# The last turn of an expert loop written out behind the loop, and a new order for the end of the kernel

## What is computed

```
for e in range(N_EXPERTS):                       # 32
    gate, up = jnp.split(z @ w_gate_up[e], 2, axis=-1)
    y = y + combine[..., e:e + 1] * ((jax.nn.silu(gate) * up) @ w_down[e])
...
return rms_norm(x + y, final_norm_g)
```

## Time and profile before

| | us |
|---|---|
| median of three runs (all: 896.52, 898.11, 900.98) | 898.11 |
| the profiled execution, its own time | 898.83 |
| the span of its trace, first to last instruction | 897.0 |
| first step of the loop begins on TensorE | 458.69 |
| last step begins on TensorE | 838.62 |
| TensorE ends that step | 868.0 |
| last matmul ends | 889.58 |

### The profile page before, as it was taken

The page is one execution under the profiler, slowest core; times in us unless marked ns, Lnnn a source line. Parts: engine busy times, 40 slices in busy tenths (PEclk is TensorE's granted clock), DMA queues, the critical chain, the costliest instruction groups (busy, mean ns, idle before and its releaser), DMA issues.

```text
span 897.0 us, 14583 instructions
## 1 busy us (share of the span) xinstructions
PE 857.0 (96%) x5764; PEld 760.9 (85%) x5764; DVE 789.7 (88%) x756; ACT 649.1 (72%) x632; POOL 11.0 (1%) x19
## 2 busy tenths in 40 slices
PE   5999999999999899969999999999999999999985
PEld 5999999999899899747788888888888888888864
DVE  5458999999877876677999999999999999999983
ACT  6563435344554474555999999999999999999973
POOL 0110000000000000001000000000000000000000
PEclk9999999999999999979999999999999999999988
DMA  9952545555424269525999999999999999999921
GB/s 380 398 189 95 199 175 188 188 188 188 174 109 177 106 236 373 212 94 202 355 412 429 425 428 430 427 430 429 427 428 430 428 427 428 430 427 429 429 102 47
DMA packets 20146, 270.64 MB, mean 302 GB/s; under 512 B 2192, under 2 KB 2448, under 8 KB 3856
## 3 DMA queue, kind: packets, MB, share of 16 engines
q1 hardware_dynamic: 19696, 268.59, 73.4%
q10 hardware_dynamic: 416, 1.57, 0.5%
HBM read 269.10 MB, written 1.05 MB: 301 GB/s over the span
## 4 chain that ended last, share of the span: by engine, by line
PE 85%; DVE 11%; issue 2%; ACT 1%; DMA 1%; DVEq 0%; SPq 0%; ACTq 0%
PE ps L1342 25%; PE ps L1356 13%; PE ps L1170 9%; PE ps L1172 9%; PE ps L1171 9%; PE ps L1329 5%; PE ps L1366 3%; DVE lo L736 2%; DVE lo L964 2%; DVE conv L823 2%; PE ps L1185 2%; PE ps L1186 2%; PE ps L1187 2%; PE ps L1447 1%; PE ps L1435 1%
## 5 line engine op out<-in xcount | busy, mean ns | idle before, releaser
L964 DVE TENSOR_TENSOR lo<-raw,hi 128x2048 fp32r<-128x2048 f32 x142 | 319.4, 2286 | 4.5 <-ACT hi L582 4.5
L582 ACT ACTIVATE hi<-raw 128x2048 fp32r<-128x2048 f32 x141 | 262.8, 1909 | 15.5 <-PE ps L1342 15.5
L400 ACT ACTIVATE hi<-raw 128x2048 fp32r<-128x2048 f32 x63 | 120.6, 1915 | 63.6 <-PE ps L1172 41.0
L736 DVE TENSOR_TENSOR lo<-raw,hi 128x2048 fp32r<-128x2048 f32 x62 | 141.7, 2289 | 28.1 <-ACT hi L400 26.7
L1170 PE MATMUL ps<-inA,hi 128*128 128x256 f32 x576 | 164.4, 285 | 1.9 <-DVE lo L736 1.1
L1171 PE MATMUL ps<-inA,hi 128*128 128x256 f32 x576 | 163.0, 283 | 0.0
L1172 PE MATMUL ps<-inA,lo 128*128 128x256 f32 x576 | 163.0, 283 | 0.0
L1342 PE MATMUL ps<-hi,xeT 128*128 128x512 f32 x384 | 154.4, 402 | 2.5 <-DVE xeT L1029 1.5
L1342 PE MATMUL ps<-lo,xeT 128*128 128x512 f32 x384 | 150.1, 391 | 0.0
L1170 PEld LDWEIGHTS ps<-inA,hi 128*128 128x128 f32 x576 | 110.5, 192 | 2.8 <-DVE lo L736 2.7
L1171 PEld LDWEIGHTS ps<-inA,hi 128*128 128x128 f32 x576 | 110.5, 192 | 0.1
(11 more groups left out here) (219 smaller groups left out, 1251.3 us busy)
## 6 DMA issues: line engine op xcount, KB each, us to landing
raw<-in_w_experts SPq DMA_DIRECT2D x96, 2048.0 KB, 12.0
raw<-in_w_dense SPq DMA_DIRECT2D x29, 2048.0 KB, 7.7
raw<-in_w_dense SPq DMA_DIRECT2D x2, 1024.0 KB, 8.1
x_sb<-in_x SPq DMA_DIRECT2D x1, 1024.0 KB, 4.9
mem_sb<-in_mem SPq DMA_DIRECT2D x1, 1024.0 KB, 15.4
x_again<-in_x ACTq DMA_DIRECT2D x1, 1024.0 KB, 4.9
out<-x SPq DMA_DIRECT2D x2, 512.0 KB, 2.7
ffn_row<-in_rows ACTq DMA_DIRECT2D x1, 512.0 KB, 7.4
```

Of the source, the lines that this page charges most:

```text
L400: return nc.scalar.activation(conv_half(hi, N), raw_half(slot, h), ACT.Copy)
L582: nc.scalar.activation(expert_half(hi, N0), raw_flat(slot, k % 2), ACT.Copy).then_inc(hi_made, 1)
L736: nc.vector.tensor_tensor(conv_half(lo, N), raw_half(slot, h), conv_half(hi, N).bitcast(f32), ALU.subtract).then_inc(lo_made, 1)
L964: nc.vector.tensor_tensor(expert_half(lo, N0), raw_flat(expert_slot(m), k % 2), expert_half(hi, N0).bitcast(f32), ALU.subtract).then_inc(l ...
```

## The change

The loop ends one turn earlier, `Fori(1, last_turn)`, and turn `last_turn` is written out behind it with the same `step`, which takes a flag. In that turn VectorE makes no selections, and in its second step (the last pair) there is no gather, no `xeT` and no `xeT_lo`. The count of the pair before comes from a second register, `turn_before`. For the last pair the order inside the step changes: VectorE computes `h` ahead of half 11 and the low part of `last_hT` directly behind it, TensorE folds up behind the first down half, and ScalarE makes silu ahead of hi of half 11. `last_hT` and `last_y` are tiles of their own. Behind the step ScalarE makes hi of halves 22 and 23 first, then `y_out` and `y_out_lo`. TensorE does down of 20, 21 and 22, then `y_remainder`, then down of 23 bank by bank, and only then `combine(0)`. The end works by half rows: `combine` of the last pair first the left 512 columns, then the right ones; four squares of 128 x 512; x is multiplied by the row of weights (`weigh`) before the root is known, and by rstd last, for tile 0 on VectorE and for tile 1 on ScalarE, which also issues the store of tile 1.

More of the change, by code:

```diff
@@ L1079, in y_out_lo, with step @@
                                         ALU.subtract).then_inc(done, 1)
-            def step(j, r):
+            def step(j, r, last_turn_=False):
                 first = isinstance(j, int)
+                last_pair = last_turn_ and r == 1
                 i = 2 * j + r
@@ L1101, in step @@
                 more(9)
-                if not start:
+                if last_pair:
+                    more(10)
+                elif not start:
                     more(10, 11)
-                dve.wait_ge(slotted, i + 1)
-                make_pick(r, slice(r + 2, r + 3) if first else bass.ds(2 * j + (r + 2), 1))
-                if not start:
+                if not last_turn_:
+                    dve.wait_ge(slotted, i + 1)
+                    make_pick(r, slice(r + 2, r + 3) if first else bass.ds(2 * j + (r + 2), 1))
+                if not start and not last_pair:
                     more(12, 13)
@@ L1380, in _, with step @@
             seed(3)
-            def step(j, r, q):
+            def step(j, r, q, turn_before=None):
                 first = isinstance(j, int)
+                last_pair = turn_before is not None and r == 1
                 i = 2 * j + r
+                pair_before = i - 1 if turn_before is None else 2 * turn_before + (r + 1)
                 start = first and i == 0
@@ L1444, in step @@
                     down(j, at_half, 11, 1)
-                pe.wait_ge(up_out, i + 1)
-                for f in range(FF // P):
-                    last = mm(G1[:, f * SLOTS:(f + 1) * SLOTS], gu_sb[:, FF + f * P:FF + (f + 1) * P], fold,
-                              start=True, stop=True, skip_group_check=True)
-                last.then_inc(up_folded, 1)
+                if not last_pair:
+                    fold_up()
             step(0, 0, slice(0, 1))
@@ L1453, in _, with last_down_half @@
             last_turn = nc.tensor.value_load(loops[0:1, 0:1], min_val=TURNS - 1, max_val=MAX_ROUNDS * TURNS - 1)
-            with pe.Fori(1, last_turn + 1) as j:
+            turn_before = nc.tensor.value_load(loops[0:1, 1:2], min_val=TURNS - 2, max_val=MAX_ROUNDS * TURNS - 2)
+            with pe.Fori(1, last_turn) as j:
                 step(j, 0, bass.ds(j % TURNS * 2, 1))
                 step(j, 1, bass.ds(j % TURNS * 2 + 1, 1))
-            y_remainder(2 * last_turn + 1)
+            step(last_turn, 0, slice(PAIRS - 2, PAIRS - 1), turn_before)
+            step(last_turn, 1, slice(PAIRS - 1, PAIRS), turn_before)
+            def last_down_half(k, x):
+                N = DENSE + 2 * STEP - 4 + k
+                h = k % 2
+                pe.wait_ge(lo_made, 2 * STEP * last_turn + (N + 1))
+                for g in range(2):
+                    for kt in range(2):
+                        for w in (hi, lo):
+                            a = kt * D + g * 512
+                            last = mm((G0, G1)[g], last_hT[:, 2 * h + kt, x, :], expert_half(w, N)[:, a:a + 512],
+                                      start=(k == 0 and kt == 0 and w is hi),
+                                      stop=(k == 3 and kt == 1 and w is lo), skip_group_check=True)
+                    if k == 3:
+                        last.then_inc(last_down, 1)
+                if k < 3:
+                    last.then_inc(half_used, 1)
             pe.wait_ge(silu_made, 2 * last_turn + 2)
```

80 lines of the change are left out of this document (51 added, 29 removed).

## The result

The changed kernel takes 887.68 us in the median of four runs (887.37 to 888.71), before 897.83 in four runs of its own (896.52 to 900.98): the ratio is 0.9883, with a 95% interval from 0.986 to 0.9906, 10.2 us. The forecast was 887.8.

A forecast was written before the change was run, and what follows sets the result against it. VectorE was taken to bound the loop. The first scaled tile moves from 892.67 to 882.4, 10.3 us; 898.83 less that is 888.5, and the median, 0.7 lower, 887.8 us, range 886.0 to 891.5.

The forecast's parts named there:

- VectorE's sum: VectorE's last turn: lo of 23 ends 5.6 us earlier, 2.08 from work left out and 3.5 from closed gaps.
- The gather at nothing: TensorE's last step: dropping two gather groups of 1.36 us gives no time itself, turning 0.2 us of slack into 2.9.
- ScalarE's order: ScalarE behind the last step: hi of 22 and 23 are 1.0 and 1.4 us early; y_out is delayed about 2 us.
- TensorE to the last matmul: TensorE from the remainder on: half 23 done at 875.35, last matmul at 879.2 against 889.6, at 2.4 GHz throughout.
- Squares: Final norm: four squares 0.61 us apart end at 880.4, 1.2 us behind the last matmul; halving the pieces gains nothing.
- The table load: ScalarE ahead of the first square: the root's table load takes 1.28 us and is now nearly uncovered.
- The first scaled tile: End of the kernel: first tile scaled 2.0 us after the last square, at 882.4 against 892.67.
- the stores: Kernel end: the span ends 4.3 us behind the first tile, as before; two queues don't shorten it.
- the clock did not fall: Rival, chance 0.07: small gaps add up, TensorE's last 30 matmuls run at 1.2 GHz, time about 892.3 us.
- The written-out turn: Rival, chance 0.02: its code queues behind weights at the loop's exit; one stop gives 898 to 900 us, two 910.
- a taken branch fewer: Loop's exit: one turn fewer saves no instruction-fetch stall, so nothing is gained there.
- 3.5 us for the gaps around hT, 22 and 23: VectorE's last pair: these gaps close, since both high parts are ready in time; 3.5 of lo of 23's 5.6 us.

The follow-up runs named there:

- leave: Kernel before with the last turn written out, without its selections and the last step's gather, xeT and xeT_lo, order otherwise unchanged: 896.46 us, ratio 0.9978.
- keep: Changed kernel with selections, gather, xeT and its low part kept in the last turn, results unread: 889.94 us, ratio 0.991 to the kernel before.
- act_order: Changed kernel with ScalarE's order behind the last step as before (y_out, hi of 22, y_out_lo, hi of 23): 895.53 us, ratio 0.998 to the kernel before.
- old_end: Changed kernel with the whole end (last combine, squares, scaling, stores) as in the kernel before: 887.13 us, ratio 0.9891 to the kernel before.
- step_order: Changed kernel with the order inside the last pair's step as before, h late again: 893.0 us, ratio 0.9943 to the kernel before.
- filled_gap: Changed kernel with the old order inside the last pair's step, plus four unused fp32 matmuls in TensorE's gap ahead of half 20: 890.55 us, ratio 0.9916.
- split: Kernel before with only the last turn written out behind the loop: 63.57 us from half 11's lo to the span's end, 897.35 us overall, ratio 0.9992.
- mid: Changed kernel with ScalarE's and TensorE's output orders and the whole end as before; left-out work and early h stay: 889.22 us, ratio 0.9909.

## Why the prediction was right

The time, 887.68 for 887.8, is right, and by its own steps.

1. *VectorE's sum.* lo of 23 was to end 5.6 us earlier; it ends 5.5 earlier against the mark. The parts were right too: leave and keep show 2.4 and 2.0 for the 2.08 that was left out.

2. *The gather at nothing.* This step is mis-sized. I said that the gather gives no time by itself and turned 0.2 us of slack into 2.9. Kept alone it costs 1.5 us: with the other work gone, TensorE would have become the bound, where it frees hi's buffers and where `h` waits for the upper fold. The sum was not hurt, since the change takes both out, and my sum needed TensorE close behind VectorE.

3. *ScalarE's order.* hi of 22 and 23 are ready 1.0 and 1.4 us before VectorE wants them (by 866.6 and 868.4, for 867.7 and 869.9), y_out near 869 and wanted at 872, as said. act_order shows what the edit guards against: 7.7 us.

4. *TensorE to the last matmul.* With the 1.3 us added that its trace was ahead, it ends at 879.4 for the forecast 879.2, down of 23 at 875.7 for 875.35. The clock stayed at 1.00 over a gap of 0.67 us, as the earlier trace rows had suggested for one of 1.5. That reading was too simple: in the same trace of before the clock is 0.50 from 382 to 384, behind a gap of 0.81 and short matmuls. The step is right in its result, and the eight traces with the early h (act_order aside) all keep 1.00 to the last matmul; but the row that it leaned on did not show that a short gap is safe.

5. *Squares.* Four at 0.58 apart, through 1.1 us behind the last matmul; the halves gained nothing, as said, and old_end has the price of the whole end, 0.2. The table load took 1.28 us with the next instruction 0.01 behind it (875.09, and 876.38 for the load's follower), and it was just covered, as the first square still waited 0.21 us for TensorE. The 2.66 us that the Trainium skill (ScalarE: Activation LUTs, What ACT_TABLE_LOAD costs) gives for a switch, its drain counted in, don't show here either.

6. *The first scaled tile* is done 1.4 us after the last root's start, at 881.2 or 882.5 with the 1.3 added, for 882.4; *the stores* end 4.4 us behind it for 4.3.

The absolute time has a little luck in it: the profiled execution took 887.39 for the forecast 888.5, and 1.3 us of that lie ahead of the change. The gain, 10.1 us for 10.3, doesn't hang on it.

The rivals: the clock did not fall in the changed part. step_order and filled_gap show that it would have, and for how much, with a gap of 3.7 us ahead of half 20, and act_order shows it for one of 5.3; behind the last step, gaps of 1.5 us and less had no fall behind them in any trace. The written-out turn was fetched under load and did not starve. That a taken branch fewer gives nothing is borne out by split, whose last turn is written out for 63.57 against 63.48. The Trainium skill (Runtime: NRT & Kernel Launch, Instruction fetch mechanics) gives a taken branch a fetch only if its target lies outside the window; for this loop no packet of the instruction queue shows one from 520 us on, so the rule gives no gain here.

What the prediction did not say is which edit carries the gain. It gave "3.5 us for the gaps around hT, 22 and 23" to the whole, and the rest to the end of TensorE. The runs give 6.1 to the order within the last pair's step together with down bank by bank, and some 2.9 of it, by the rows of leave and mid, come by way of the clock.

## What to carry to other kernels

At the end of a pipelined loop, look at who waits for the last item's own results: in the loop, the next item's work covers that wait, and behind it nothing does. Computing the last item's intermediate three pieces earlier was worth 4 us here with all else in place, and 6 together with finishing the last sums bank by bank; leaving out the work for an item that doesn't exist was worth 2.4, and rearranging the final norm 0.2. When two engines' orders are changed together, as the high parts and the remainder here, one without the other can cost more than either gives; and a gap of TensorE of 3.7 us cost 1.5 us on top of the work that stood still, because of the clock behind it.

## What I had not expected of the hardware

Dummy matmuls pay: four fp32 matmuls of 512 columns into a gap of 3.7 us made the kernel 1.5 us faster, by holding the granted clock at 1.00 where it was 0.50. They ran as eight passes of 0.46 us, 3.65 together. The instruction queues carry code near the exit of the loop, five packets between 820 and 875 us, the DMA engines being full until about 854. VectorE shows no wait for them, and split, with the same turn written out, takes the time of before; for the loop itself they carried nothing from 520 to 820 us, although the loop's branch was taken again and again. And the part ahead of the experts varied by 1.3 us between executions of the same instructions, as the granted clock fell to 0.50 in three traces of fourteen and not in the others; that is as much as several of the effects tried here.
